# A decoder step on one Trainium2 core: the last attention stores, decode weights, the routing stage's first loads and the experts' gathers are reordered

## The reference

```python
mod = silu(c) @ w_ada + b_ada                      # six vectors of 1024, one set per row of c
sh1, sc1, gt1, sh2, sc2, gt2 = split(mod, 6)
h = rmsnorm(x, g_n1) * (1 + sc1) + sh1
q, k, v, u_val, u_gate = split(h @ w_in)
branches = [branch(q, k, v, rel_bias, w, d) for w, d in ((128, 1), (512, 4), (2048, 16))]
att = combine_branches(branches)                   # each gives its numerator, maximum m and sum l
cext = concatenate([conv_buf, u_val * sigmoid(u_gate)])
conv = silu(layernorm(dwconv(cext, conv_w, conv_b), ln_g, ln_b))
x = x + gt1 * (concatenate([att, conv]) @ w_out)
h2 = rmsnorm(x, g_n2) * (1 + sc2) + sh2
lg = h2 @ w_rg + b_rg                              # 4 groups: the best one
le = (h2 @ w_re + b_re)[its 8 experts]             # the two best, softmax weights
x = x + gt2 * sum(weight * ((silu(h2 @ w1) * (h2 @ w3)) @ w2))
y = rmsnorm(x, g_final)
```

## Time and profile before

| | |
|---|---|
| runs, median | 2343.29 us (2343.26, 2343.29, 2346.63) |
| profiled execution | 2340.75 us, span 2339.2 us |
| mean granted clock of PE | 0.929 of 2.4 GHz |
| PE busy, weight loads | 1981.8 us (85%), 1598.6 us (68%) |
| DVE, ACT, POOL busy | 1610.3, 1073.1, 576.4 us |
| DMA | 553.66 MB, mean 237 GB/s |

### The profile page before, as it was taken

One profiled execution on the slowest core, in us unless ns is written; L12 is line 12 of the kernel. 1 busy time (PEld: TensorE's weight loads), 2 busy tenths in 40 slices (PEclk: granted clock), 3 DMA queues, 4 the chain that ended last, 5 costly groups with the idle time before them and its releaser, 6 DMA issues. The chain is left out here.

```text
span 2339.2 us, 40473 instructions
## 1 busy us (share of the span) xinstructions
PE 1981.8 (85%) x13004; PEld 1598.6 (68%) x13005; DVE 1610.3 (69%) x3110; ACT 1073.1 (46%) x2055; POOL 576.4 (25%) x564
## 2 busy tenths in 40 slices
PE   5999999997999988439999749899999998999910
PEld 3788888886777766217888637788777876878700
DVE  2568888888566667628999648766455675548778
ACT  2311111112777778005444237665445564547533
POOL 1024444440111112202555321101100111010066
PEclk8999999999999999669999869999999998999955
DMA  8855555554646466774787449968575977679777
GB/s 264 271 194 198 198 196 198 181 187 140 224 133 205 132 223 233 237 239 155 241 274 265 139 166 347 364 243 305 190 273 199 344 276 282 250 250 377 289 294 292
DMA packets 221017, 553.66 MB, mean 237 GB/s; under 512 B 28477, under 2 KB 43413, under 8 KB 219768
## 3 DMA queue, kind: packets, MB, share of 16 engines
q1 hardware_dynamic: 176464, 435.12, 53.2%
q0 software_dynamic: 25440, 76.21, 9.0%
q10 hardware_dynamic: 19024, 41.18, 5.0%
HBM read 457.38 MB, written 167.63 MB: 267 GB/s over the span
## 5 line engine op out<-in xcount | busy, mean ns | idle before, releaser
L597 DVE SCALAR_TENSOR_TENSOR ARENA<-ARENA,TAPW 128x512 f32<-128x512 f32 (+3 forms) x493 | 293.3, 673 | 0.0
L2383 DVE TENSOR_TENSOR LO<-WIDE,HI 128x2048 fp32r<-128x2048 f32 x128 | 284.5, 2283 | 4.3 <-ACT HI L2302 4.3
L2302 ACT CAST HI<-WIDE 128x2048 fp32r<-128x2048 f32 x128 | 240.1, 1910 | 56.0 <-DMA WIDE<-in_w_expert_gate 37.2
L423 POOL TENSOR_TENSOR MS<-SSQ,K 128x1 f32<-128x1 f32 x17 | 170.4, 10021 | 291.6 <-ACT H L466 291.6
L2383 DVE TENSOR_TENSOR LO<-W2E,HI 128x2048 fp32r<-128x2048 f32 x64 | 143.7, 2285 | 92.3 <-ACT HI L2302 92.3
L716 PE MATMUL PJ<-WIN_H,HTH 128*128 128x512 f32 x680 | 173.9, 399 | 15.0 <-ACT HTH L472 11.7
L1027 ACT ACTIVATE PR<-SBX,NM 128x256 f32<-128x256 f32 (+1 forms) x384 | 171.9, 455 | 2.3 <-DVE NM L961 2.3
L720 PE MATMUL PJ<-WIN_H,HTL 128*128 128x512 f32 x680 | 168.4, 390 | 0.0
L724 PE MATMUL PJ<-WIN_L,HTH 128*128 128x512 f32 x680 | 168.0, 389 | 0.0
L498 ACT ACTIVATE ARENA<-PJ 128x512 f32<-128x512 f32 x51 | 30.4, 598 | 292.9 <-PE PJ L724 292.9
L716 PEld LDWEIGHTS PJ<-WIN_H,HTH 128*128 128x128 f32 x680 | 128.1, 191 | 46.4 <-ACT HTH L472 15.9
(11 more groups left out here) (338 smaller groups left out, 4348.0 us busy)
## 6 DMA issues: line engine op xcount, KB each, us to landing
WIDE<-in_w_expert_gate SPq DMA_DIRECT2D x64, 1024.0 KB, 6.6
WIDE<-in_w_expert_up SPq DMA_DIRECT2D x64, 1024.0 KB
W2E<-in_w_expert_down SPq DMA_DIRECT2D x64, 1024.0 KB
expert_rows<-YE ACTq DMA_DIRECT2D x40, 512.0 KB, 5.6
expert_rows<-NOROWS POOLq DMA_DIRECT2D x11, 1536.0 KB, 11.7
WAD<-in_w_ada SPq DMA_DIRECT2D x16, 1024.0 KB, 7.1
X<-in_x_prompt SPq DMA_DIRECT2D x31, 512.0 KB
QN<-q_rows SPq DMA_DIRECT2D x48, 256.0 KB, 3.0
```

What stands on the lines that cost most here:

```text
L423: pool.tensor_tensor(MS[:], SSQ[:], const("eps"), ALU.add).then_inc(ms_ready, 1)
L597: ins = nc.vector.scalar_tensor_tensor(out=out, in0=src, scalar=tap, in1=out, op0=ALU.mult, op1=ALU.add)
L2302: nc.scalar.copy(HI[n][:, cols], raw[n][:, cols]).then_inc(hi_ready[n], 1)
L2383: nc.vector.tensor_tensor(LO[n][:, cols], raw[n][:, cols], HI[n][:, cols], ALU.subtract).then_inc(lo_ready[n], 1)
```

## The change

Six groups of edits.

1. *Attention's end.* The stores of the last four blocks (ML and O) are issued by SP behind its last loads; POOL's loop ends four blocks earlier. ACT waits for their semaphores before it writes O again.
2. *Ring of w_ada.* WAD is now a buffer of attention and decode; BIAS[0] and BIAS[1] are its slots 0 and 1. ACT loads halves 0 and 1 in the attention at blocks 33 and 35, when the branch that uses the slot is done, and half 2 at block 14; the other 13 halves are loaded in the decode stage as before.
3. *Decode.* SP issues the bias rows BAD first, then DROWS, then halves 3 to 5, each of which waits for the use of half 0 to 2. PE does modulation chunks 0 and 1 ahead of the first product with S0X, and ACT's copies follow.
4. *Head of routing.* The table `lower` and its 512 KB load are gone. ACT issues CC(0) and LN only. SP issues NB(0), STAT(0), WO, and then in round -1 CC(1), the modulation rows and G2, NB(1), STAT(1), WR and BR. On DVE, GAIN moves behind tile 0 in round 0, LNH behind the first MIX, on its own semaphore. PE waits for WR at the first logits instead of the first projection, and in round -1 turns MIX(0) before CC(1).
5. *Table.* The two products with `lower` become two copies and five shifted additions (a running sum by doubling) in SUMS.
6. *Experts.* POOL fetches the slot lists of the first two small blocks and gathers both ahead of its loop; in the loop the next small block is fetched after the run's experts, and only its gather waits for PE to have turned the one before. ACT casts and DVE computes LO of up(0) ahead of the first small block. In an expert's last block DVE computes the first half of LO of the next gate ahead of G (GE), the rest behind as before. PE's wait for the small tile's copy (sx_ready) moves from every block to the end of a small one.

```diff
@@ attention @@
-        BIAS = [sb(f"BIAS{b}", [P, HEADS, (2 if b < 2 else 1) * P]) for b in range(3)]
+        BIAS = [state["ada"][:, b].rearrange("p k (n x) -> p (k n) x", x=2 * P) for b in range(2)] + [sb("BIAS2", [P, HEADS, P])[:]]
@@ SP, behind its last round @@
+                for q in range(4):
+                    g = Round(STEPS - 1, q, STEPS - 1)
+                    r = g.at - 8 * SEGMENT
+                    sp.wait_ge(nm_ready, g.count(0, 2, 2))
+                    sp.wait_ge(exp_done, g.count(0, 2, 2))
+                    sp.dma_start(dilated(dr["stat"][2], DILATIONS[2], r, 0, P), ML[q][:]).then_inc(last_ml_out, 16)
+                    sp.wait_ge(o_taken, g.count(0, 1, 1))
+                    sp.dma_start(dilated(dr["num"][2], DILATIONS[2], r, 0, P), O[q % 2][:]).then_inc(last_o_out[q % 2], 16)
@@ POOL @@
-                with pool.Fori(2 * SEGMENT, 3 * SEGMENT) as s:
+                with pool.Fori(2 * SEGMENT, 3 * SEGMENT - 1) as s:
@@ ACT, ahead @@
+                    for x, at in enumerate((33, 35, 14)):
+                        if g == at:
+                            if x < 2:
+                                act.wait_ge(mx_done, 8 * (x + 1) * 4 * SEGMENT)
+                            act.dma_start(state["ada"][:, x], t["w_ada"][0].rearrange("(k p) n -> p k n", p=P)[:, ks, col:col + 512]).then_inc(state["ada_in"][x], 16)
@@ decode, SP @@
-                    if x >= RINGS:
-                        sp.wait_ge(w_used, x + 1 - RINGS)
+                    sp.wait_ge(w_used, x + 1 - RINGS)
-                sp.dma_start(R[:], dr["dec"].rearrange("n b c -> b n c")).then_inc(rows_in, 16)
-                for x in range(RINGS):
-                    weights(x)
+                for x in range(RINGS, 2 * RINGS):
+                    weights(x)
@@ decode, PE @@
+                modulation(range(2))
                 pe.wait_ge(new_spread, 1)
                 nc.tensor.matmul(N0P, S0X[:].rearrange("b a h -> b (a h)"), const("ones", DEC)[:, 0:1], start=True, stop=True).then_inc(new_psum, 1)
-                modulation(range(2))
@@ routing, SP in a round @@
+                    if isinstance(i, int) and i == -1:
+                        for dst, part in ((GATE, 2), (GAIN, 4), (SHIFT, 3)):
+                            sp.dma_start(dst[:, 0], dr["mod"][DEC:DEC + 1, part * D:(part + 1) * D].to_broadcast([P, D])).then_inc(mods_in, 16)
+                            sp.dma_start(dst[0:DEC, 1], dr["mod"][0:DEC, part * D:(part + 1) * D]).then_inc(mods_in, 16)
+                        sp.dma_start(G2[:], t["g_norm2"].to_broadcast([P, D])).then_inc(mods_in, 16)
...
+                    if isinstance(i, int) and i == -1:
+                        sp.dma_start(WR[:, :, 0:GROUPS], t["w_router_group"][0].rearrange("(k p) n -> p k n", p=P)).then_inc(weights_in, 16)
+                        sp.dma_start(WR[:, :, GROUPS:], t["w_router_expert"][0].rearrange("(k p) n -> p k n", p=P)).then_inc(weights_in, 16)
+                        sp.dma_start(BR[:, 0:GROUPS], t["b_router_group"].to_broadcast([P, GROUPS])).then_inc(bias_in, 16)
+                        sp.dma_start(BR[:, GROUPS:], t["b_router_expert"].to_broadcast([P, NEXP])).then_inc(bias_in, 16)
@@ routing, table on DVE @@
-                    below(RUN, SMALL1)
-                    below(FROM, FULL)
+                    then(nc.vector.tensor_copy(SUMS[0][:, 0, NEXP + 1:], SMALL1[:, 0:NEXP - 1]))
+                    then(nc.vector.tensor_copy(SUMS[0][:, 1, NEXP + 1:], FULL[:, 0:NEXP - 1]))
+                    for n in range(5):
+                        now, to = SUMS[n % 2], SUMS[1 - n % 2]
+                        then(nc.vector.tensor_tensor(to[:, :, NEXP:], now[:, :, NEXP:], now[:, :, NEXP - 2 ** n:2 * NEXP - 2 ** n], ALU.add))
@@ experts, POOL @@
                 def fetch_small(e, n):
-                    pool.wait_ge(sx_turned, n)
+                    pool.wait_ge(sx_in, pool.snap(n * 16 - 16))
                     pool.dma_start(IDXS[:], dr["slot"][ds(slot, T), :]).then_inc(sidx_in, 16)
                     pool.wait_ge(sidx_in, n * 16)
+                    pool.wait_ge(sx_turned, n)
                     pool.indirect_dma_start(XGS[:], None, dr["h2"], bass.IndirectOffsetOnAxis(ap=IDXS[:].bitcast(U32), axis=0)).then_inc(sx_in, 16)
...
-                    fetch_small(entry(pool, 5, g + 1, 0, LAST), g + 1)
                     with pool.Fori(head, behind) as e:
+                        fetch_expert(e)
+                    fetch_small(entry(pool, 5, g + 2, 0, LAST), pool.snap(g + 2))
@@ experts, DVE block_ @@
+                    if following is not None:
+                        lower(0, following, (0,))
                     dve.wait_ge(s_ready, b + 2)
...
                     rest_x(b + 1)
-                    for n in range(2):
-                        split(n)
+                    if following is not None:
+                        lower(0, following, (1,))
+                        lower(1, following)
```

More of the change, by code:

```diff
@@ L108, in constant_columns @@
             parts["ownhead"][r, r % HEADS * DH:(r % HEADS + 1) * DH] = 1.0
-    parts["lower"] = np.tile((np.arange(NEXP)[None, :] < np.arange(NEXP)[:, None]).reshape(1, -1), (P, 1))
     parts["zero"] = np.zeros((P, NEXP * CAP // P))
@@ L157, in decoder_step @@
             state["dec_in"] = [lasting(f"dec_{x}_in") for x in "qkv"]
+            state["ada"] = both.enter_context(nc.sbuf_tensor("WAD", [P, ADA_RING, KD // 2, 512], F32))
+            state["ada_in"] = [lasting(f"dec_ada_in{n}") for n in range(ADA_RING)]
             if stop_after >= 2:
@@ L1274, in _ @@
                 sp.dma_start(OWN[:], t["constants"][:, at:at + width]).then_inc(own_in, 16)
-                for x in range(RINGS, 2 * NCH):
+                for x in range(2 * RINGS, 2 * NCH):
                     weights(x)
@@ L1622, in _ @@
                 pool.memset(NOROWS[:], 0.0).then_inc(norows_set, 1)
+                for n in range(2):
+                    pool.memset(SUMS[n][:], 0.0).then_inc(preset, 1)
                 def normalise(i):
@@ L2378, in _, with lower @@
             def _(dve):
-                def lower(n, e):
-                    for half in range(2):
+                def lower(n, e, halves=(0, 1)):
+                    for half in halves:
                         dve.wait_ge(hi_ready[n], e * 2 + half + 1)
```

130 lines of the change are left out of this document (70 added, 60 removed).

## The result

The changed kernel takes 2288.3 us (median of 4 runs, 2286.6 to 2289.4) against 2343.28: a ratio of 0.9762 (95% interval 0.9745 to 0.9779), 55.0 us less where 41.6 were forecast. Run again beside the last experiments it took 2286.65 (5 runs), ratio 0.9744 (0.9717 to 0.977). It is faster, as forecast, and by more: a third more than the sum said, at the very edge of the range (2288.0), and the second series lies beyond it.

The account below looks back on a forecast made before the run. Six stages that don't overlap, each bound by its own waits (drain, weights, router bias, gathers, full DMA): −8.2 + 1.5 − 2.6 − 16.5 − 0.8 − 3 − 5 − 7 = −41.6, so 2301.7 us at the median; range 2288 to 2325.

Parts of the forecast that it names:

- Stores on SP: Attention's end: the last four blocks' stores leave POOL, whose drain is then covered, so decode starts earlier; −8.2 us.
- Loads in the attention: Attention: three 1 MB loads of w_ada halves, two in a stretch with DMA at 0.93 of full, cost +1.5 us.
- Decode: Decode stage: early weight waits go and modulation no longer stands before the scores' turn; −2.6 us.
- DVE's score chain is unchanged: Decode stage: DVE's scores end as before, so PE turns them at about 986.6 instead of 988.41, −1.8 us.
- The two DMA waits behind the turn: Decode stage: PE's two waits for DMA after turning the scores go, 0.8 us.
- Routing: Routing stage: second projection at T+35.5 instead of T+52.0, −16.5 us (best −19, worst −10); smaller table operations, −0.8.
- Experts' head: Expert stage's start: the first gathered tile XG comes about one slot-list landing earlier; −3 us (0 to −7).
- Early stretch: Experts, 1400 to 1500 us: about 3 MB of loads moves into earlier free DMA time; −5 us (−1 to −8).
- Lone experts: Single-expert runs: the slot list no longer waits for PE, the gather comes 5 us earlier; −7 us (−3 to −7.2).
- LO ahead of G: Each expert's last block: DVE's first half of the next LO fits while GE waits for PE; taken at nothing.
- rival (c): Experts: the early LO half delays G, up to 2.28 us in each of 31 experts, so 2372; chance 0.12.
- (b): Rival: decode gives back all 8.1 us of preloaded traffic, experts' early stretch all 8: 2293; chance 0.08.

## Why the prediction was wrong, point by point

- **Stores on SP, −8.2.** Right: 8.9 by the run that puts them back. POOL's drain was covered and SP's was 7 ns.
- **Loads in the attention, +1.5.** Too high: 0 within the spread. The stretch at 0.93 of full had room: with the loads it stood at 1.01, and PE was busy 16.44 of 20 us there, 16.35 before.
- **Decode, −2.6.** It did not come: +0.7 in this profile, −0.2 in the means. That the run without the loads is 2.7 slower is no proof of the price, since it has the new order and not the old one. Three steps failed. "DVE's score chain is unchanged" is one: its product for ST waits 1.1 us longer for LBD, since SP now issues the small inputs behind halves that wait for a slot, so the turn came 34.7 us after the stage's first DMA, not 33.7 (35.5 before). I followed PE's waits for weights and not what SP's moved issues do to the small inputs. The two DMA waits behind the turn were to go, but one of 2.00 us stands in their place, and OD starts 10.4 us behind the turn as before. And that OD would take 1.75 us more at a lower clock was not thought of. −0.8 and +1.75 is all but 0.2 of the +0.7. Taking the other five profiles of the same code, the turn comes 36.0 to 37.3 us into the stage, against 35.9 to 36.5 in the stage as before.
- **Routing, −16.5 and −0.8.** Right in its path and sum: T + 35.57, 17.0 in all, with two errors of 0.9 and 0.8 us that cancel.
- **Experts' head, −3.** 1.0. The new fetch gives 2.8, but casts and LO of the up weights ahead of the small block cost 1.9; the forecast let them be free.
- **Early stretch, −5.** Right: 5.3. The forecast's edit gives it alone, and so does the half of LO, so in the kernel after it has two causes at once. The limit of about 358 GB/s that the Trainium skill gives ("DMA: Bandwidth & Descriptors", Specifications) does not hold here: the trace's two windows after have 394 and 404 GB/s, loads and stores together.
- **Lone experts, −7.** 4.5 in this profile, 2.7 and 3.4 in two others, nothing in three more. The forecast counted the earlier slot list of the small tile, but its gather, the register loads behind it and the second slot list still stand ahead of XG on POOL, and PE comes 2.7 us sooner. That its issue can wait for an LO operation of DVE was not in the sum.
- **LO ahead of G, at nothing.** This is the step that failed most, by 18.7 us less 3.1. I looked only at what the moved operation delays (G, rival (c)) and not at what it had delayed where it stood: GS, at the end of the same four LO operations. The row on it, nine waits for DVE's GS of up to 1.7 us, 13.7 in all, was in the trace before. Of the 18.7 us some 11 are these waits at the seven boundaries, and most of the rest the lower clock behind them. Rival (c) named a real cost, but small: in the six blocks that follow a boundary PE now waits 0.8 to 1.1 us for GE, which it did not before, and needs 19.1 to 19.4 us instead of 18.3 to 19.3, 3.1 in all.

Sum by profile: −1.0 − 5.3 − 18.7 − 4.5 + 3.1 = −26.4 for the experts. The range ended where the result fell, because an operation priced at nothing had been given no bound on the side of a gain. No rival covered what came either: (b) with the best bound of the routing head gives 2290.7.

## What to carry to other kernels

A moved operation has two ends: ask who waits behind its new place, and who waited behind its old one. List the waits of the whole stage by what they wait for, also those under 2 us that come back nine times, before an edit is taken at nothing. Data that is loaded ahead is worth nothing until the engine that frees its slot is not standing at something else: look at the order in which that engine waits. And where a gather's issue can fall into a long operation of DVE, put it well ahead instead of hoping for the draw.

## What the runs showed of the hardware

- POOL's drain at a stage's end takes time with all its DMAs landed, and more the more of them it issued in the stage: 0.67 us in the decode stage with none, 1.71 in the set-up with 20, 3.75 in the routing stage with 45, 7.25 and 7.90 in the attention with 88 and 96 (82 ns for each of the eight stores between them), 11.8 in the experts with 102, most of them gathers and slot lists. SP's, behind stores of the same shape, took 7 ns.
- A wait of 1.7 us on PE, with one of 0.45 behind the next product, was followed in some places and not in others by the granted clock's lower level, and then cost 3.4 us instead of 1.7. OD, the same 48 matmuls, took 5.36 us at a granted clock of 1.00 and 7.11 to 7.42 at 0.75 to 0.72. The wait ahead of it doesn't decide alone: behind one of 1.48 us it took 7.42, behind one of 1.50 in another kernel 5.36.
- The issue of an indirect gather on POOL that starts inside an LO operation of DVE (2.3 us) ends 0.85 us behind that operation's end: it grew from 1.0 to up to 3.1 us, and the landing from 6.5 to 8.6 us behind its start.
- The DMA engines moved 394 and 404 GB/s, loads and stores together, over 20 us each.
